# Value sums of a banded attention: two 256-column corner matmuls in place of two 512-column ones, and the sums gated on GpSimd

## The reference, cut to what matters

```python
def band_mask(n_blocks):
    qi = jnp.arange(WINDOW)[:, None]
    s = jnp.arange(2 * WINDOW)[None, :]
    diff = WINDOW + qi - s
    ...
    valid = (diff >= 0) & (diff < WINDOW)
    return valid[None] & (key_pos >= 0)
...
    o = jnp.einsum("bnkgqs,bnskd->bnqkgd", probs.astype(v_band.dtype), v_band)
    o = o.reshape(B, S, Q_HEADS * HEAD_DIM)
    return (o * jax.nn.silu(z)) @ w_out
```

## Time and profile before

| | |
|---|---|
| time, median of 3 runs (lowest, highest) | 2231.12 us (2231.07, 2231.17) |
| span of the profiled execution | 2230.9 us |
| own time of the profiled execution | 2231.1 us to a tenth, as all three runs: 0.2 us above the span |
| PE busy, share of the span | 2163.5 us, 97% |
| DVE, ACT, POOL busy | 1436.8, 1032.7, 1037.3 us |
| attention steps, first to last value sum | about 1548 to 2191 us |

### The profile page before, as it was taken

The page is one execution under the profiler, slowest core; times in us unless marked ns, Lnnn a source line. Parts: engine busy times, 40 slices in busy tenths (PEclk is TensorE's granted clock), DMA queues, the critical chain, the costliest instruction groups (busy, mean ns, idle before and its releaser), DMA issues.

```text
span 2230.9 us, 28791 instructions
## 1 busy us (share of the span) xinstructions
PE 2163.5 (97%) x10410; PEld 1808.6 (81%) x10410; DVE 1436.8 (64%) x1815; ACT 1032.7 (46%) x1898; POOL 1037.3 (46%) x636
## 2 busy tenths in 40 slices
PE   5999999999999999999999999999999999999998
PEld 4887778788888878888787888887888888888887
DVE  6966548757476864554974653867676657657764
ACT  4334445634545644445644445434444434434442
POOL 2556775845553865544684555440222232232222
PEclk9999999999999999999999999999999999999999
DMA  9888899785559795557876565989677797787554
GB/s 344 307 300 309 310 319 343 236 309 174 201 189 334 277 322 173 197 192 279 312 277 247 179 211 206 353 341 361 226 282 243 260 342 251 268 313 274 196 203 170
DMA packets 244782, 592.86 MB, mean 266 GB/s; under 512 B 20928, under 2 KB 96800, under 8 KB 244256
## 3 DMA queue, kind: packets, MB, share of 16 engines
q1 hardware_dynamic: 241680, 585.71, 72.8%
q10 hardware_dynamic: 2960, 5.30, 0.7%
HBM read 461.96 MB, written 119.54 MB: 261 GB/s over the span
## 4 chain that ended last, share of the span: by engine, by line
PE 74%; DMA 7%; POOL 6%; DVE 5%; ACT 3%; DVEq 2%; POOLq 1%; issue 1%; SPq 1%; ACTq 0%
PE ps L2272 22%; PE ps L2274 22%; PE ps L2273 22%; POOL w_lo L1110 3%; DMA w_raw<-in_a_w_in 2%; PE ps L2477 2%; POOL cbl L1129 1%; PE ps L2527 1%; PE ps L2526 1%; PE ps L2552 1%; DMA zo<-tt 1%; DVE yb L2018 1%; DMA w_raw<-a_weights_combined 1%; DMA r<-b_input 1%; ACT w_hi L1304 1%
## 5 line engine op out<-in xcount | busy, mean ns | idle before, releaser
L1110 POOL TENSOR_TENSOR w_lo<-w_raw,w_hi 128x1024 fp32r<-128x1024 f32 x244 | 650.4, 2684 | 568.8 <-ACT w_hi L1304 568.8
L1304 ACT ACTIVATE w_hi<-w_raw 128x1024 fp32r<-128x1024 f32 x260 | 271.7, 1057 | 413.8 <-DMA w_raw<-in_a_w_in 370.2
L2272 PE MATMUL ps<-h,w_hi 128*128 128x512 f32 x1024 | 403.2, 394 | 10.2 <-POOL w_lo L1110 9.4
L2274 PE MATMUL ps<-h,w_lo 128*128 128x512 f32 x1024 | 398.9, 390 | 0.0
L2273 PE MATMUL ps<-h,w_hi 128*128 128x512 f32 x1024 | 398.7, 389 | 0.0
L1249 POOL TENSOR_SCALAR_AFFINE_SELECT pt<-pt 128x512 fp32r<-128x512 f32 x128 | 82.2, 642 | 395.4 <-ACT pt L1666 338.9
L2272 PEld LDWEIGHTS ps<-h,w_hi 128*128 128x128 f32 x1024 | 192.2, 188 | 55.5 <-POOL w_lo L1110 14.7
L2274 PEld LDWEIGHTS ps<-h,w_lo 128*128 128x128 f32 x1024 | 192.2, 188 | 40.6
L2273 PEld LDWEIGHTS ps<-h,w_hi 128*128 128x128 f32 x1024 | 192.4, 188 | 38.9 <-issue 0.2
L2272 PE MATMUL ps<-r,w_hi 128*128 128x512 f32 x480 | 191.7, 399 | 3.8 <-ACT kvf L1608 2.3
L2274 PE MATMUL ps<-r,w_lo 128*128 128x512 f32 x480 | 187.7, 391 | 0.0
(11 more groups left out here) (268 smaller groups left out, 4636.8 us busy)
## 6 DMA issues: line engine op xcount, KB each, us to landing
w_raw<-in_a_w_in SPq DMA_DIRECT2D x256, 256.0 KB, 3.6
w_hi<-b_weights_split SPq DMA_DIRECT2D x104, 512.0 KB, 4.4
w_lo<-b_weights_split SPq DMA_DIRECT2D x104, 512.0 KB, 5.8
w_raw<-in_a_w_in SPq DMA_DIRECT2D x52, 512.0 KB, 4.9
w_raw<-in_a_w_out SPq DMA_DIRECT2D x48, 512.0 KB, 5.7
w_hi<-v_weights_combined SPq DMA_DIRECT2D x48, 512.0 KB, 4.0
w_lo<-v_weights_combined SPq DMA_DIRECT2D x48, 512.0 KB, 5.1
w_hi<-a_weights_combined SPq DMA_DIRECT2D x32, 512.0 KB, 6.3
```

What stands on the lines that cost most here:

```text
L1110: g.tensor_tensor(wlo[p][:, rows_], raw[p][:, rows_], whi[p][:, rows_].bitcast(F32), ALU.subtract).then_inc(w_lo, 1)
L1304: s_.activation(whi[p][:, rows_], raw[p][:, rows_], ACT.Copy).then_inc(w_hi, 1)
L2272: t_.matmul(dst_, stat[0], mov[0], start=start, stop=False)
L2274: return t_.matmul(dst_, stat[1], mov[0], start=False, stop=stop)
```

## The change

The base of a value sum is no longer one block for all keys. vst now holds the own block's values for keys 0 to 63 and the previous block's for keys 64 to 127. With that base only two corners are wrong: keys 0 to 63 against queries 0 to 63 where the key is above the query, and keys 64 to 127 against queries 64 to 127 where it is not. Each corner is 64 keys by 64 queries by 4 heads, so 256 columns. High parts and rests of the corner's probabilities are laid on the two halves of the partitions (p_edge), against difference tiles (edge_low, edge_up) that hold the same 64 rows twice, and one matmul does both.

```diff
-                t_.matmul(bank(7), dst[:, blk, kh, :], pt[:, 2, :], start=False, stop=False)
-                t_.matmul(bank(7), dst[:, blk, kh, :], pt[:, 3, :], start=False, stop=True).then_inc(pv_full, 1)
+                pe.wait_ge(edge_lo, at("edge_lo", g, kh + 1))
+                pe.wait_ge(pt_masked, a + 1)
+                by_query = bank(7).rearrange("p (h q) -> p h q", h=4)
+                t_.matmul(by_query[:, :, 0:HEAD], edge_low[:, blk, kh, :], p_edge[:, 0, :], start=False, stop=False)
+                t_.matmul(by_query[:, :, HEAD:P], edge_up[:, blk, kh, :], p_edge[:, 1, :], start=False, stop=True) \
+                    .then_inc(pv_full, 1)
```

```diff
-                    v.tensor_tensor(pt[:, 1, :], bank(6), pt[:, 0, :].bitcast(F32), ALU.subtract).then_inc(pt_lo, 1)
-                if 0 <= a - 2 < ATT:
-                    gated_output(a - 2)
+                    v.tensor_tensor(pt[:, 1, :], bank(6), pt[:, 0, :].bitcast(F32), ALU.subtract).then_inc(pt_all, 1)
+                    turned_p = bank(6).rearrange("p (h q) -> p h q", h=4)
+                    high = pt[:, 0, :].rearrange("p (h q) -> p h q", h=4).bitcast(F32)
+                    v.tensor_tensor(p_edge[64:P, 0].rearrange("p (h q) -> p h q", h=4), turned_p[0:64, :, 0:HEAD],
+                                    high[0:64, :, 0:HEAD], ALU.subtract)
+                    v.tensor_tensor(p_edge[0:64, 1].rearrange("p (h q) -> p h q", h=4), turned_p[64:P, :, HEAD:P],
+                                    high[64:P, :, HEAD:P], ALU.subtract).then_inc(pt_lo, 1)
```

```diff
-                        s_.activation(ot[0:64], low[:, :, 0, :], ACT.Copy)
-                        s_.activation(ot[64:P], low[:, :, 1, :], ACT.Copy).then_inc(o_low, 1)
+                        for there, half in ((ot, low), (obt, high)):
+                            s_.activation(there[0:64], half[:, :, 0, :], ACT.Copy, scale=0.5)
+                            last = s_.activation(there[64:P], half[:, :, 1, :], ACT.Copy, scale=0.5)
+                        last.then_inc(o_copied, 1)
```

POOL per slot, in this order: `gated_output(a - 2)` (an add and a multiply, 128x256), `mask(a - 1)` (four selects of 64x256 in place of two of 128x512), `normalise(a)`. Once per group and head it also makes the rests of the edge tiles:

```diff
+            def gated_output(a):
...
+                pool.drain()
+                pool.wait_ge(o_copied, a + 1)
+                g.tensor_tensor(obt[:], obt[:], ot[:], ALU.add)
+                pool.drain()
+                pool.wait_ge(zg_done, at("zg_done", q, f0 + 2))
+                gated = zg[:, f0:f0 + 2, P * blk:P * blk + P]
+                g.tensor_tensor(gated, obt[:], gated, ALU.mult).then_inc(o_done, 1)
+            def edge_rest(g_, kh):
+                pool.drain()
+                pool.wait_ge(kv_hi_done, at("kv_hi_done", g_, kh + 1))
+                for n, (edge, here) in enumerate(((edge_up, slice(64, P)), (edge_low, slice(0, 64)))):
+                    for there in (slice(0, 64), slice(64, P)):
+                        last = g.tensor_tensor(edge[there, :, kh, HEAD:P], df[here],
+                                               edge[here, :, kh, 0:HEAD].bitcast(F32), ALU.subtract)
...
+                last.then_inc(edge_lo, 1)
```

More of the change, by code:

```diff
@@ L468, in yoco_kernel @@
         bsh = place("bsh", sp_at + 8 * K, [GROUPS * P], F32)
-        dst = place("dst", sp_at, [NC, KVH, P], F32R)
+        edge_up = place("edge_up", sp_at, [NC, KVH, P], F32R)
         kw = place("kw", sp_at + 4 * K, [T], F32)
@@ L1245, in mask @@
             def mask(a):
[L1247 to L1252, removed]
@@ L1253, in mask, with kept @@
-                last.then_inc(pt_masked, 1)
+                def kept(there, in_, low):
+                    heads = there.rearrange("p (h q) -> p h q", h=4)
+                    if low:
+                        return g.affine_select(out=heads, in_=in_, compare_op=ALU.is_ge, fill=0.0, base=0,
+                                               pattern=[[0, 4], [1, HEAD]], channel_multiplier=-1)
+                    return g.affine_select(out=heads, in_=in_, compare_op=ALU.is_gt, fill=0.0, base=0,
+                                           pattern=[[0, 4], [-1, HEAD]], channel_multiplier=1)
@@ L1283, in _ @@
                     normalise(a)
-                for pc in slot:
+                    if a % STEPS == 3:
+                        edge_rest(a // STEPS, 1)
+                for k, pc in enumerate(slot):
                     tasks(pc)
+                if s and keys_in(s - 1) is not None:
+                    edge_rest(keys_in(s - 1), 0)
             for pc in range(B_PIECES, B_PIECES + 6):
@@ L1646, in kv_round @@
                 s_.activation(ks[rows_, kh, 0, P:5 * P], kw[rows_, :], ACT.Copy)
-                s_.activation(vst[:, 1:5, kh, 0:HEAD], kvf[:, 1:5, cols_], ACT.Copy)
-                s_.activation(dst[:, :, kh, 0:HEAD], df[:], ACT.Copy).then_inc(kv_hi_done, 1)
+                s_.activation(vst[0:64, :, kh, 0:HEAD], kvf[0:64, 1:5, cols_], ACT.Copy)
+                s_.activation(vst[64:P, :, kh, 0:HEAD], kvf[64:P, 0:4, cols_], ACT.Copy)
+                for there in (slice(0, 64), slice(64, P)):
+                    s_.activation(edge_low[there, :, kh, 0:HEAD], df[0:64], ACT.Copy)
+                    last = s_.activation(edge_up[there, :, kh, 0:HEAD], df[64:P], ACT.Copy)
+                last.then_inc(kv_hi_done, 1)
             def kv_double(g, kh):
@@ L2551, in p_transposes @@
                 for n in range(4):
-                    last = t_.transpose(bank(6, P, P * n), pp[:, a % 2, n, 1:P + 1], ident[:])
+                    last = t_.transpose(bank(6, P, P * n), pp[a % 2][:, n, 1:P + 1], ident[:])
                 last.then_inc(pt_full, 1)
```

81 lines of the change are left out of this document (46 added, 35 removed).

## The result

The changed kernel takes 2243.23 us, median of 4 runs (2242.61 to 2244.32), against 2231.14 us for the kernel before, 4 runs (2231.07 to 2233.95). The ratio is 1.0059, 95% interval 1.0045 to 1.0073. The profiled execution took 2243.17 us with a span of 2241.4, against a span of 2230.9 before: +10.5. The time lies 14 us above the forecast's range, on the other side of no change.

What follows compares the result with a forecast made beforehand. PE was taken to set the time, busy 637.1 of 647.0 us. Terms: -13.8 (columns) + 3.4 + 0.9 + 0.8 (renewals) + 0.5 (DVE-POOL meetings) + 0.5 (clock) = -7.7 us, from 2231.12 to 2223.4 us; 8-in-10 range 2217.3 to 2229.0.

Steps and rivals of the forecast that it cites:

- the columns: Value sums on PE: two matmuls per step shortened to 256 columns save 0.216 us per step, 13.8 us over 64 steps.
- the clock: PE's matmuls after the new wait at step 28 may run at 1.2 GHz: +0.5 us (bounds 0 and 1.4).
- the price of POOL's operations behind the renewal: POOL after ACT's rounding: subtractions and gate operations at 0.52 us each, the whole chain 5.3 us (bounds 3.3 and 9.3).
- ordinary steps have 2 us of cover left: Value sums of ordinary steps: the corner chain takes 1.35 us against 1.25 before, an exchange, leaving 2 us of cover.
- step 28: Key and value renewal in group 2: the third value matmul moves by 3.4 us (bounds 1.4 and 7.3).
- rival B: The renewals of keys and values are hidden too, giving 2217 to 2220 us; chance 0.24.
- Step 10: Key and value renewal in group 1: the third value matmul comes 0.9 us later (bounds 0 and 4.9).
- step 45: Key and value renewal in group 3: hidden, with 0.5 us to spare (upper bound 3.4).
- The head 1 rounds: DVE's kv_rest waits 1.24 us more for ACT, four times: 0.2 us each, 0.8 in all (bounds 0 and 4).
- The gate product on POOL and ACT's two copies: Every step's gate add and multiply on POOL and two more ACT copies of 0.38 us: hidden in most steps, nothing.
- Rival C: Waits at steps 28, 10 and 45 plus clock eat nearly all, 12 us: about 2230 us, no change; chance 0.15.
- Rival D: POOL becomes the pace and each of 64 steps waits; at 0.5 us a step +18 us, 2249; chance 0.07.

Runs made afterwards that it cites:

- e12: The changed kernel without DVE's two corner rests and POOL's two selects on them in every step, renewals unchanged; ratio 1.0001 to the kernel before.
- e4: The kernel before with only the gate product moved to POOL and four ACT copies, value sums still 512 columns; ratio 1.0002 to the kernel before.
- e10: The changed kernel with corner roundings and rests put off and value sums one projection piece later; ratio 0.9967 to the kernel before.
- e2: The changed kernel with ACT's corner roundings and POOL's corner rests put off to later slots; ratio 1.0008 to the kernel before.

## Why the prediction was wrong

From span to span the forecast was -7.7 us and +10.5 came. The difference of 18.2 us splits, but for rounding, into 1.2 for the columns, 11.2 for the waits (16.8 where 5.6 were forecast), 9.1 for the clock (9.6 where 0.5 was), and -3.2 outside the stretch, which nothing explains. Three steps failed: the price of POOL's operations behind the renewal, the claim that ordinary steps have 2 us of cover left, and the half microsecond for the clock behind all new waits.

- **The columns, -13.8 us: right.** The rest of the stretch fell by 12.6 us in 63 steps, 0.20 us each (11 to 13 us in the other kernels with corners), and the strided output costs nothing.
- **The mechanism at step 28: right; the size, +3.4 us, was off.** POOL's chain from the end of ACT's rounding to the third matmul took 7.4 us, not 5.3: four subtractions and two products cost 0.72 to 0.99 us each and not 0.52, 1.6 us more in all, and the gaps between operations came to 0.9 us, not 0.5. ACT's rounding grew by 1.8 us, not 1.24 (3.10 us for seven copies), since its 64x256 copies stand 0.43 us apart and not 0.31. The two misses make 2.1 + 0.6 = 2.7 us, which takes the term to 6.1; PE waited 5.49 us there, 0.42 before. The slip is in the scaling: the selects were read between two rows and came out right, while the products were scaled from the one row of 512 columns as if an operation of no columns took no time. The lower bound of the chain was wrong as a sum too: 6 x 0.4 + 4 x 0.29 + 0.5 is 4.1 us, not 3.3, so the lower bound at step 28 was 2.1 us, and rival B had less for it than was said.
- **Step 10, +0.9, and step 45, nothing: mis-sized by the same prices.** With 2.7 us more each they would be 3.6 and, after the 0.5 us to spare, 2.2; they waited 3.4 and 2.1 us. All three lie within their bounds, but one price enters all three and moves them together, and the range did not carry this.
- **The head 1 rounds, +0.8 us: the mechanism right, the size not.** In group 2 DVE waited 3.04 us for ACT's rounds, the gate behind them came late, and PE waited 1.83 us with 1.5 us of halved clock.
- **"In an ordinary step 2 us of cover are left": the step that failed in kind.** It counted the chain from L2234 on and took L2234's own time as given. In slots in which ACT rounds queries or copies `kvf`, the chain starts later because ACT's two copies and DVE's two rests stand ahead of its parts. That gave the wait of step 20, and 1.0 us more at each of two waits for `kvf` (2.12 where it was 1.16 and 1.15). For DVE's part e12 shows it; ACT's part is read from the rows of step 20, and no run took it alone.
- **The clock, +0.5 us: +9.6 was measured.** One slow stretch was priced where six new ones came, 1.3 to 1.7 us each, behind waits of 1.3 to 5.5 us. The rule of the Trainium skill weighed there (TensorE: Matmul & The Clock Gate, HAM oscillation), that idle gaps between bursts bring the halved clock back, was the better guide than my 0.5: the trace agrees at those six places. It doesn't at every wait: of two waits of 2.12 us for `kvf` the one at 2009.40 us was followed by a slow stretch and the one at 1816.75 was not. So such a stretch is a risk to be priced with each wait, not a certainty.
- **The gate product on POOL and ACT's two copies, nothing: right by themselves** (e4).
- **Rival C** had the right places and priced them at 12 us: they came to about 15, 11.0 of waits (0.4 before) and 4.8 of halved clock. The other 11 us came at places that it did not name. **Rival D**, the main case that was slower, was wrong in its reason: POOL isn't the pace, it waits for others in nearly every step.

In e10's order the waits are 3.0 us above the kernel before and the halved clock is level with it, and the time is 0.9967 of before, or 7.4 us of 2231. That this is nearly the forecast's 7.7 is luck: it is another order, with other waits, and shows that the columns' gain can be had, not that the sum was right.

## What to carry to other kernels

A once-per-group job put into an in-order queue ahead of a per-step job is as long a wait as its whole chain, and it should stand behind the step's work as soon as nothing reads it for some steps. That move alone took +0.6% to +0.1% (e2); together with value sums one piece later it came to -0.3% (e10). Price a wait on TensorE with the slow stretch that may follow it, and let all terms that share an unseen unit price move together in the range. Don't scale a short operation's time by its columns from one long row; read it between two rows. When two additions are each taken for hidden, ask for the slots in which they meet: e4 cost nothing, and leaving out either half of the corner work made the slowdown vanish, though not the whole loss.

## What the runs showed of the hardware

- POOL's two-input operations: 1.04 us for 128x512, 0.72 to 0.74 for 128x256, about 0.75 for 64x256 (two in 1.49 to 1.53 us). Half the columns save 0.3 us, half the partitions nothing. An estimate from the first two sizes is 0.42 us plus 1.2 ns for a column. The selects take 0.64 us for 128x512, 0.41 for 64x256 and 0.29 for 128x128, which is an estimated 0.17 us plus 0.9 ns for a column.
- ACT's copies of 64x256 from SBUF start 0.41 to 0.44 us apart in a row of six, with no overlap. The two copies of 128x256 that they replace started 0.30 to 0.31 us apart, at 0.40 us each. What ends the overlap was not tried.
- The halved clock does not follow the length of the wait alone. In the changed kernel a wait of 1.32 us at step 20, with 0.65 us for a DMA behind it, was followed by it, and so was one of two waits of 2.12 us for `kvf`; in e12 one of 2.6 us at step 10 and in e10 one of 2.1 us for `kvf` were not. What decides was not tried.
